# State-space tables made ahead and kept in DRAM, small matmuls of two pairs side by side, and a shorter final norm

## The chip, the cores and the metric

The kernel runs on one core of a Trainium2 chip. The metric is the device time of one execution in microseconds (us), the median over several runs. A trace of one profiled execution of the kernel before is at hand; its times count from the start of its span.

## The reference, cut to what matters

One layer of a streaming encoder over 512 tokens of width 2048: a projection, an attention that picks keys by an indexer, a state-space layer (S5) beside it, gates, an output projection, and a final RMSNorm. The parts that the change touches:

```python
bu_re = einsum("blgc,gpc->blgp", ug, bb_re)     # 32 groups: 16 channels in, 64 complex states each
bu_im = einsum("blgc,gpc->blgp", ug, bb_im)
# x[l] = lambda * x[l-1] + bu[l], lambda complex, one for each group and state
_, _, x_re, x_im = associative_scan(s5_combine, (lam_re, lam_im, bu_re, bu_im), axis=1)
y = einsum("blgp,gcp->blgc", x_re, c_re) - einsum("blgp,gcp->blgc", x_im, c_im) + d * ug
...
x = x + (gates[:, :, 0] * y_a + gates[:, :, 1] * y_b) @ w_out
out = x * rsqrt(mean(x * x, axis=-1) + EPS) * g_final
```

## The kernel before

Activations lie transposed in SBUF: features over the partitions, the 512 tokens along the free axis. Each large product runs as three matmuls in fp32r: high part by high part, low by high, high by low (lines 393 to 395; the output projection has its own, lines 646 to 648). A weight unit is 1 MB: SP loads it into one of three slots (`load`, line 299), ScalarE writes its high part (`w_hi`, line 673), VectorE the rest (`w_lo`, line 947). A unit of a projection is 48 matmuls of 128x512. All engines run orders written out by hand, tied by semaphores.

The stages follow each other on TensorE: indexer and q, k, v; `attgate` and `u` with the attention's small steps between their matmuls (35 steps, `attention_step`); `attout` (16 tiles of 24 matmuls, which ScalarE copies to `ya`); `merge0` (16 tiles of 48); `ssmgate`, `glu`, `ssmout`, `merge1`; `out` in two halves of 1024 columns.

The state-space layer runs inside `merge0`. Its 32 groups are 16 pairs; a pair fills 128 partitions (2 groups of 64 states). For pair j:

- `bu_of` on TensorE: six matmuls that contract over 32 rows (fp32r) into the two banks `pair_bank`, just ahead of a tile.
- VectorE turns the result back by the angle of each token (four products with the table `e_tab` of cosines and sines, two sums), scans along the tokens with the magnitude alone (`tensor_tensor_scan`, twice), and turns it forward again (four products, two sums) into `x_ri`.
- `y_of` on TensorE: two plain fp32 matmuls of 128 rows by 32 columns into a 32-partition strip of `sum_bank`, in the middle of a tile.

The table of pair j+1 is made during pair j by doubling: `e_start` copies 32 columns of `e_base`, and `e_double` goes 32 to 64 to 128 to 256 to 512. ScalarE makes the products with the sine (`e_scale`, line 840), VectorE two `scalar_tensor_tensor` for each doubling (lines 1228 and 1229). GpSimd multiplies each `merge0` gate into `ya` (line 376).

At the end, as each bank of the second half of `out` is done, VectorE adds it to the residual `res` (line 1352), ScalarE squares it (line 919), and for each tile t of 128 tokens the inverse norm is found (lines 922, 923, 1335). Then VectorE scales and weights 1344 of the 2048 columns (line 1337), while GpSimd weights the other 704 (line 383) for ScalarE to scale (line 907). SP sends both parts out (lines 344 and 346).

## Time and profile before

| | |
|---|---|
| Median of 3 runs | 1221.36 us (1220.9 to 1221.44) |
| The profiled execution's own time | 1219.88 us |
| Its span | 1218.0 us |
| TensorE busy | 1188.4 us (98%) |
| VectorE busy | 728.1 us (60%) |
| ScalarE busy | 417.3 us (34%) |
| GpSimd busy | 42.9 us (4%) |
| Mean granted TensorE clock | 0.997 of full |

The span is what the trace covers; the execution's own time is 1.88 us longer, and the median of the runs is 1.48 us above that. The profile names groups of instructions by line and tile. A matmul's row gives the time until its end, 0.39 us for 128x512, while the next starts 0.23 us later, so what a matmul costs in a full stream is read from start to start.

### The profile page before, as it was taken

The page shows a single profiled execution, that of the slowest core. Times are in us where ns is not written, and L with a number is a line of the kernel's source. Part 1 is how long each engine was busy: PE and PEld are TensorE (multiplying, and loading weights), DVE is VectorE, ACT ScalarE, POOL GpSimd, SP SyncE. Part 2 cuts the span into 40 slices and gives each one's busy share as a digit, 9 for nine tenths or more (in the row PEclk, how much of TensorE's full clock was granted, in tenths as well). Part 3 has the DMA queues.
Part 4 walks back from the last instruction along what each step waited for, and adds up shares of the span by engine and source line. Part 5 has one row for each costly group of instructions (what it writes and reads, how often), then busy time and mean ns, then how long its engine had stood idle before and what let it go on. Part 6 is the DMA issues. An engine that isn't in the chain of part 4 may idle for free.

```text
span 1218.0 us, 13219 instructions
## 1 busy us (share of the span) xinstructions
PE 1188.4 (98%) x5357; PEld 959.2 (79%) x5357; DVE 728.1 (60%) x1253; ACT 417.3 (34%) x558; POOL 42.9 (4%) x32
## 2 busy tenths in 40 slices
PE   5999999999999999999999999999999999999996
PEld 4999888887777888876666666788888888887885
DVE  5887479999456452469999999543223343523224
ACT  7432333323355432233233424233321222313114
POOL 3000000000000000000101011000000000000002
PEclk9999999999999999999999999999999999999998
DMA  7344232333221143322222222233333333255323
GB/s 241 104 120 122 71 100 73 80 93 104 69 70 36 51 116 104 104 72 77 80 78 75 69 70 69 70 104 104 95 81 102 104 104 91 85 175 204 103 70 138
DMA packets 167276, 118.07 MB, mean 97 GB/s; under 512 B 10456, under 2 KB 158256, under 8 KB 166064
## 3 DMA queue, kind: packets, MB, share of 16 engines
q1 hardware_dynamic: 160608, 116.34, 33.1%
q10 hardware_dynamic: 6608, 0.90, 0.4%
q8 instruction: 42, 0.69, 0.2%
q14 instruction: 18, 0.15, 0.0%
HBM read 113.03 MB, written 4.19 MB: 96 GB/s over the span
## 4 chain that ended last, share of the span: by engine, by line
PE 84%; DVE 12%; ACT 2%; DMA 1%; issue 1%; POOLq 0%; SPq 0%; DVEq 0%; ACTq 0%
PE bank L393 21%; PE bank L394 20%; PE bank L395 20%; PE bank L646 4%; PE bank L647 4%; PE bank L648 4%; DVE w_lo L947 2%; DVE score L1052 2%; DVE small L1051 2%; PE bank L545 1%; PE bank L526 1%; PE bank L583 1%; PE bank L584 1%; DVE score L1040 1%; DMA xt<-in_x 1%; PE bank L598 1%
## 5 line engine op out<-in xcount | busy, mean ns | idle before, releaser
L393 PE MATMUL bank<-act_hi,w_hi 128*128 128x512 f32 (+1 forms) x1088 | 424.5, 390 | 2.7 <-DVE w_lo L947 2.7
L394 PE MATMUL bank<-act_lo,w_hi 128*128 128x512 f32 (+1 forms) x1088 | 417.3, 384 | 0.0
L395 PE MATMUL bank<-act_hi,w_lo 128*128 128x512 f32 (+1 forms) x1088 | 417.0, 383 | 0.0
L947 DVE TENSOR_TENSOR w_lo<-w_raw,w_hi 128x2048 fp32r<-128x2048 f32 x96 | 219.8, 2290 | 195.6 <-ACT w_hi L673 194.7
L393 PEld LDWEIGHTS bank<-act_hi,w_hi 128*128 128x128 f32 x1088 | 204.3, 188 | 58.1 <-issue 19.2
L395 PEld LDWEIGHTS bank<-act_hi,w_lo 128*128 128x128 f32 x1088 | 204.3, 188 | 38.7
L394 PEld LDWEIGHTS bank<-act_lo,w_hi 128*128 128x128 f32 x1088 | 204.5, 188 | 34.2
L673 ACT ACTIVATE w_hi<-w_raw 128x2048 fp32r<-128x2048 f32 (+1 forms) x97 | 184.5, 1902 | 106.4 <-DMA w_raw<-in_w_out 105.3
L840 ACT ACTIVATE e_prod<-e_tab,rot 128x64 f32<-128x64 f32 (+1 forms) x64 | 31.8, 496 | 149.9 <-DVE e_tab L1229 90.9
L646 PE MATMUL bank<-w_hi,act_hi 128*128 128x512 f32 x192 | 74.7, 389 | 0.0
L647 PE MATMUL bank<-w_lo,act_hi 128*128 128x512 f32 x192 | 74.7, 389 | 0.0
L648 PE MATMUL bank<-w_hi,act_lo 128*128 128x512 f32 x192 | 74.7, 389 | 0.0
L1324 DVE TENSOR_TENSOR gate<-gate,yb 128x512 f32<-128x512 f32 x16 | 11.1, 692 | 97.3 <-ACT gate L679 97.3
L679 ACT ACTIVATE gate<-bank,g_cols 128x512 f32<-128x512 f32 x16 | 11.0, 688 | 134.1 <-PE bank L395 134.1
L743 ACT ACTIVATE relu<-bank 128x256 f32<-128x256 f32 (+2 forms) x48 | 23.6, 491 | 90.9 <-PE bank L494 84.7
L393 PE MATMUL bank<-a_hi,w_hi 128*128 128x512 f32 x128 | 49.9, 390 | 0.0
L395 PE MATMUL bank<-a_hi,w_lo 128*128 128x512 f32 x128 | 49.8, 389 | 0.0
L394 PE MATMUL bank<-a_lo,w_hi 128*128 128x512 f32 x128 | 49.8, 389 | 0.0
L376 POOL TENSOR_TENSOR ya<-ya,gate 128x512 f32<-128x512 f32 x16 | 23.3, 1457 | 710.0 <-ACT gate L852 710.0
L1040 DVE SCALAR_TENSOR_TENSOR score<-relu,w_idx,score 128x256 f32<-128x256 f32 (+2 forms) x45 | 27.8, 618 | 28.9 <-ACT relu L743 27.8
L646 PEld LDWEIGHTS bank<-w_hi,act_hi 128*128 128x128 f32 x192 | 36.0, 188 | 7.5
L647 PEld LDWEIGHTS bank<-w_lo,act_hi 128*128 128x128 f32 x192 | 36.0, 188 | 7.5
(241 smaller groups left out, 1383.5 us busy)
## 6 DMA issues: line engine op xcount, KB each, us to landing
w_raw<-in_w_in SPq DMA_DIRECT2D x68, 1024.0 KB, 5.6
w_raw<-in_w_out SPq DMA_DIRECT2D x16, 1024.0 KB, 5.5
w_raw<-in_w_att_out SPq DMA_DIRECT2D x8, 1024.0 KB, 5.5
xt<-in_x SPq DMA_DIRECT2D x4, 1024.0 KB, 7.9
w_raw<-in_w_ssm_out SPq DMA_DIRECT2D x4, 1024.0 KB, 5.1
res<-in_x SPq DMA_DIRECT2D x4, 1024.0 KB, 11.5
out_dram<-res SPq DMA_DIRECT2D x4, 672.0 KB, 3.1
out_dram<-res SPq DMA_DIRECT2D x4, 352.0 KB, 3.4
```

Source lines behind the costliest of these rows:

```text
L393: nc.tensor.matmul(out_ap, wh, x_hi[k], start=(j == 0), stop=False)
L394: nc.tensor.matmul(out_ap, wh, x_lo[k], start=False, stop=False)
L395: last = nc.tensor.matmul(out_ap, wl, x_hi[k], start=False, stop=(j == n - 1))
L646: nc.tensor.matmul(out_ap, mh, w_hi[:, slot, w], start=(k == 0), stop=False)
L647: nc.tensor.matmul(out_ap, mh, w_lo[:, slot, w], start=False, stop=False)
L648: last = nc.tensor.matmul(out_ap, ml, w_hi[:, slot, w], start=False, stop=(k == KD - 1))
L673: nc.scalar.activation(w_hi[:, u % SLOTS, 0:n_el], w_raw[:, u % SLOTS, 0:n_el], ACT.Copy).then_inc(high_done, 1)
L840: nc.scalar.activation(e_prod[:, :, 0:n], e_tab[:, j % 2, :, 0:n], ACT.Copy, scale=rot[:, 1, 4 + i, j:j + 1]).then_inc(e_scaled, 1)
L947: v.tensor_tensor(w_lo[:, u % SLOTS, :], w_raw[:, u % SLOTS, :], w_hi[:, u % SLOTS, :].bitcast(F32), ALU.subtract).then_inc(split_done, 1)
L1040: ins = v.scalar_tensor_tensor(scores[b], r, w, scores[b], ALU.mult, ALU.add)
L1051: link(v.max(small[:, 12:20], scores[b]))
L1052: link(v.match_replace(scores[b], small[:, 12:20], scores[b], REPLACED))
```

## The change

Tables. `e_base` is built ahead of the attention's first step. The tables of pairs 0 to 7 are made during the attention's steps, one doubling a step (`e_point`), ScalarE and VectorE sharing the work as before. Those of pairs 8 to 15 are made whole by VectorE at the start of `attout` (`e_whole`). ScalarE's queue stores each table in DRAM (`store_e`, 512 KB), and in `merge0` SP loads them back (`load_e`).

Small matmuls. `bu_of` and `y_of` work for two pairs at a time, every second tile, their matmuls alternating between the pairs: in `bu_of` the two pairs have different strips of 32 rows and different banks, in `y_of` different strips of 32 output columns. `x_ri` has two buffers. VectorE takes over GpSimd's gate product.

Final norm. The last two weight units are taken together, so that banks are done one at a time with 12 matmuls each. VectorE scales the first 1024 columns, weighted ahead in the first half, and weights the other 1024 while ScalarE squares; ScalarE scales them. GpSimd has no part.

```diff
+        e_prod = at("e_prod", r1 + 22 * KB, [2, SEQ // 2])
+        e_made = [at("e_made0", r1 + 28 * KB, [2, SEQ]), at("e_made1", r4, [2, SEQ])]
+            def load_e(j):
+                if j >= 2:
+                    sp.wait_ge(x_ready, j - 1)
+                else:
+                    sp.wait_ge(tile_done, TILE0["merge0"])
+                sp.dma_start(e_tab[:, j % 2, :, :], e_dram[j]).then_inc(e_loaded[j % 2], 16)
+            for stored_ in e_stored:
+                sp.wait_ge(stored_, 16 * PAIRS // 2)
+            for n, u in enumerate([*units("merge0"), *units("ssmgate")]):
+                load(u, KD, w_in_cols(COL_MERGE + P * n if n < KD else COL_SG + P * (n - KD)))
+                if n == 2:
+                    load_e(0)
+                    load_e(1)
+                if 4 <= n < PAIRS + 2:
+                    load_e(n - 2)
...
-            for j in range(KD):
-                pool.wait_ge(tile_free, TILE0["merge0"] + j + 1)
-                pool.tensor_tensor(ya[:, j, :], ya[:, j, :], gate[:, j % 2, :], ALU.mult).then_inc(gate_used, 1)
...
             def y_of(j):    
-                pe.wait_ge(x_ready, j + 1)
-                nc.tensor.matmul(out_ap, c_w[:, 0, q, 32 * jj:32 * jj + 32], x_ri[:, 0, :], start=True, stop=False)
-                nc.tensor.matmul(out_ap, c_w[:, 1, q, 32 * jj:32 * jj + 32], x_ri[:, 1, :], start=False, stop=True
+                pe.wait_ge(x_ready, j + 2)
+                for r in range(2):
+                    for p in (0, 1):
+                        cols_ = slice(32 * (jj + p), 32 * (jj + p) + 32)
+                        last = nc.tensor.matmul(sum_bank[q % 2][cols_, :], c_w[:, r, q, cols_], x_ri[:, p, r, :],
+                                                start=(r == 0), stop=(r == 1))
             def bu_of(j):
-                if j >= 1:
+                if j >= 2:
                     pe.wait_ge(bu_used, j)
...
-                if 1 <= n <= PAIRS:
+                if n % 2 == 1 and n < PAIRS:
                     bu_of(n - 1)
-                                              lambda k: y_of(n - 2) if k == KD // 2 and 2 <= n <= PAIRS + 1 else None)
+                                              lambda k: y_of(n - 3) if k == KD // 4 and n % 2 == 1 and 3 <= n <= PAIRS + 1 else None)
...
+            def store_e(j):
+                act.wait_ge(e_grown, 5 * (j + 1) if j < E_EARLY else 4 * E_EARLY + j + 1)
+                act.dma_start(e_dram[j], e_made[j % 2][:, :, :]).then_inc(e_stored[j % 2], 16)
+            def e_point(n):
+                if n % len(E_LEVELS) == 0 and n:
+                    store_e(n // len(E_LEVELS) - 1)
+                if n < len(E_LEVELS) * E_EARLY:
+                    j, l = n // len(E_LEVELS), E_LEVELS[n % len(E_LEVELS)]
+                    act.wait_ge(e_grown, n + j + 1)
+                    nc.scalar.activation(e_prod[:, :, 0:2 ** l], e_made[j % 2][:, :, 0:2 ** l], ACT.Copy, scale=rot[:, 1, l - 1, j:j + 1]
+                                         ).then_inc(e_scaled, 1)
...
+                act.wait_ge(bank_taken, 8 + 2 * t + 2)
+                link(nc.scalar.activation(square_out[:, 0, :], res[:, t, HALF + 512:D], ACT.Square, accum_out=small[:, 176 + t:177 + t]))
+                nc.scalar.activation(small[:, 184 + t:185 + t], small[:, 176 + t:177 + t], ACT.Sqrt, bias=small[:, 180 + t:181 + t],
+                                     scale=1.0 / D).then_inc(squares_done, 1)
                 act.wait_ge(scale_ready, t + 1)
+                nc.scalar.activation(res[:, t, HALF:D], fin[:, t % 2, :], ACT.Copy, scale=small[:, 188 + t:189 + t]
...
+            def e_whole(j):
+                er, ei = e_made[j % 2][:, 0, :], e_made[j % 2][:, 1, :]
+                dve.wait_ge(e_stored[j % 2], 16 * (j // 2))
+                link(v.tensor_copy(e_made[j % 2][:, :, 0:E_BASE], e_base[:, :, j, :]))
+                for l in E_LEVELS:
+                    n_, rr, ri = 2 ** l, rotors[l][0][:, j:j + 1], rotors[l][1][:, j:j + 1]
+                    link(v.tensor_scalar(e_prod[:, :, 0:n_], e_made[j % 2][:, :, 0:n_], ri, None, ALU.mult))
+                    a = mark(v.scalar_tensor_tensor(er[:, n_:2 * n_], er[:, 0:n_], rr, e_prod[:, 1, 0:n_], ALU.mult, ALU.subtract))
+                    last = v.scalar_tensor_tensor(ei[:, n_:2 * n_], ei[:, 0:n_], rr, e_prod[:, 0, 0:n_], ALU.mult, ALU.add)
+            e_whole(E_EARLY)
+            e_whole(E_EARLY + 1)
+            for i in (0, 1, 2):
+                low_through(UNIT0["attout"] + i + 2)
+                e_whole(E_EARLY + 2 * i + 2)
+                e_whole(E_EARLY + 2 * i + 3)
...
-                if nxt:
-                    e_double(j + 1, 5)
+                dve.wait_ge(tile_free, TILE0["merge0"] + j + 1)
+                v.tensor_tensor(ya[:, j, :], ya[:, j, :], gate[:, j % 2, :], ALU.mult).then_inc(gate_used, 1)
...
+                v.tensor_scalar(res[:, t, 0:HALF], res[:, t, 0:HALF], small[:, 188 + t:189 + t], None, ALU.mult).then_inc(final_done, 1)
```

In TensorE's order, this is where the first `bu_of` stands in the kernel before, between a tile into bank 1 and the next into bank 0 (banks 2 and 3 are `pair_bank`):

```order
L395 MATMUL bank1<-act_hi_49,w_lo_52 128x512
L598 MATMUL bank2<-u_hi_96,b_hi_87 128x512
L599 MATMUL bank2<-u_lo_97,b_hi_87 128x512
L600 MATMUL bank2<-u_hi_96,b_lo0_115 128x512
L598 MATMUL bank3<-u_hi_96,b_hi_87 128x512
L599 MATMUL bank3<-u_lo_97,b_hi_87 128x512
L600 MATMUL bank3<-u_hi_96,b_lo1_86 128x512
L393 MATMUL bank0<-act_hi_49,w_hi_53 128x512
```

The same place in the changed kernel (banks 4 and 5 are `turn_bank`, which take the second pair):

```order
L616 MATMUL bank2<-u_hi_97,b_hi_90 128x512
L616 MATMUL bank4<-u_hi_97,b_hi_90 128x512
L618 MATMUL bank2<-u_lo_98,b_hi_90 128x512
L618 MATMUL bank4<-u_lo_98,b_hi_90 128x512
L620 MATMUL bank2<-u_hi_97,b_lo0_116 128x512
L620 MATMUL bank4<-u_hi_97,b_lo0_116 128x512
L616 MATMUL bank3<-u_hi_97,b_hi_90 128x512
L616 MATMUL bank5<-u_hi_97,b_hi_90 128x512
L618 MATMUL bank3<-u_lo_98,b_hi_90 128x512
L618 MATMUL bank5<-u_lo_98,b_hi_90 128x512
L620 MATMUL bank3<-u_hi_97,b_lo1_89 128x512
L620 MATMUL bank5<-u_hi_97,b_lo1_89 128x512
```

Twelve matmuls of two pairs stand where six of one pair stood, and the place ahead of the following tile is empty.

The end of TensorE's order in the kernel before, the last two of the eight banks:

```order
L646 MATMUL bank6<-w_hi_53,act_hi_49 128x512
L647 MATMUL bank6<-w_lo_52,act_hi_49 128x512
L648 MATMUL bank6<-w_hi_53,act_lo_50 128x512
L646 MATMUL bank6<-w_hi_53,act_hi_49 128x512
L647 MATMUL bank6<-w_lo_52,act_hi_49 128x512
L648 MATMUL bank6<-w_hi_53,act_lo_50 128x512
L646 MATMUL bank7<-w_hi_53,act_hi_49 128x512
L647 MATMUL bank7<-w_lo_52,act_hi_49 128x512
L648 MATMUL bank7<-w_hi_53,act_lo_50 128x512
L646 MATMUL bank7<-w_hi_53,act_hi_49 128x512
L647 MATMUL bank7<-w_lo_52,act_hi_49 128x512
L648 MATMUL bank7<-w_hi_53,act_lo_50 128x512
```

In the changed kernel twelve matmuls go into bank 7 there, after twelve into bank 6; so the last but one bank is done twelve matmuls ahead of the end, not six.

On ScalarE's order, the start of `attout` in the changed kernel (L709 copies a tile to `ya`, L808 is a store of `store_e`); before, the copies and the `w_hi` stand there alone:

```order
L709 ACTIVATE ya<-bank 128x512
L703 ACTIVATE w_hi<-w_raw 128x2048
L808 DMA e_tables<-e_made_117 128x1024
L709 ACTIVATE ya<-bank 128x512
L808 DMA e_tables<-e_made_118 128x1024
L709 ACTIVATE ya<-bank 128x512
```

Each of the first eight copies now has a store behind it, which waits for VectorE's table, so the next copy waits for that too.

## Rows read from the trace of the kernel before

**Rows 1.** The page, busy time and share of the span, TensorE.

```profile
PE 1188.4 (98%) x5357; PEld 959.2 (79%) x5357; DVE 728.1 (60%) x1253; ACT 417.3 (34%) x558; POOL 42.9 (4%) x32
```

**Rows 2.** Timeline of TensorE around one `bu_of`: start us, us, engine, line, operation.

```profile
620.09 0.39 PE L395 MATMUL bank<-act_hi,w_lo 128*128 128x512 f32 x1
...
620.41 0.49 PE L598 MATMUL bank<-u_hi,b_hi 32*128 32x512 f32 x1
...
621.99 0.19 PEld L393 LDWEIGHTS bank<-act_hi,w_hi 128*128 128x128 f32 x1 [0.36 <-issue]
621.99 0.50 PE L393 MATMUL bank<-act_hi,w_hi 128*128 128x512 f32 x1
622.10 0.19 PEld L394 LDWEIGHTS bank<-act_lo,w_hi 128*128 128x128 f32 x1
...
622.33 0.39 PE L394 MATMUL bank<-act_lo,w_hi 128*128 128x512 f32 x1
```

**Rows 3.** Timeline of TensorE around one `y_of`.

```profile
628.02 0.39 PE L395 MATMUL bank<-act_hi,w_lo 128*128 128x512 f32 x1
...
628.34 1.04 PE L583 MATMUL bank<-x_ri,c_w 128*32 128x512 f32 x2
629.22 1.02 PE L584 MATMUL bank<-x_ri,c_w 128*32 128x512 f32 x2
...
630.51 0.40 PE L394 MATMUL bank<-act_lo,w_hi 128*128 128x512 f32 x1
```

**Rows 4.** Timeline of VectorE: one pair from its first product to its last doubling.

```profile
622.20 0.69 DVE L1255 TENSOR_TENSOR prod<-bank,e_tab 128x512 f32<-128x512 f32 x1 [0.26 <-PE bank L600]
622.81 0.68 DVE L1256 TENSOR_TENSOR prod<-bank,e_tab 128x512 f32<-128x512 f32 x1
...
635.59 0.48 DVE L1229 SCALAR_TENSOR_TENSOR e_tab<-e_tab,rot,e_prod 128x256 f32<-128x256 f32 x1
```

**Rows 5.** Groups by line, VectorE, 529.9 to 766.6: busy us, mean ns, idle before.

```profile
L1229 DVE SCALAR_TENSOR_TENSOR e_tab<-e_tab,rot,e_prod 128x32 f32<-128x32 f32 (+3 forms) x60 | 20.2, 337 | 0.0
```

**Rows 6.** Timeline of the attention's steps, in brackets idle time and what ended it.

```profile
352.17 1.28 ACT L762 ACT_TABLE_LOAD   x1 [0.69 <-DVE small L1144]
...
354.38 0.71 PE L545 MATMUL bank<-pT,v_tok 128*128 128x128 f32 x4 [1.34 <-ACT pT L772]
...
400.15 0.49 DVE L1152 TENSOR_SCALAR probs<-probs,small 128x512 f32<-128x512 f32 x1
```

**Rows 7.** Attention's window: PE, PEld, DVE, ACT, POOL busy, clock, DMA share, GB/s.

```profile
314.00:434.00 120.00, 118.50 (x628) 96.67 (x627) 62.69 (x208) 58.00 (x122) 0.00 (x0) 1.00 0.19 54
```

**Rows 8.** The page, ScalarE's group for the tables.

```profile
L840 ACT ACTIVATE e_prod<-e_tab,rot 128x64 f32<-128x64 f32 (+1 forms) x64 | 31.8, 496 | 149.9 <-DVE e_tab L1229 90.9
```

**Rows 9.** Timeline of VectorE: the attention's first step, and later `e_base`, first and last.

```profile
324.06 0.29 DVE L1141 CUSTOM_DVE_ANT_0 probs<-bank,bias 128x128 f32<-128x128 f32 x1 [9.72 <-PE bank L526]
...
502.70 0.07 DVE L1192 MEMSET e_base<- 128x16 f32 x1
...
511.46 0.42 DVE L1096 TENSOR_TENSOR e_base<-b_raw 128x256 f32<-128x256 f32 x1
```

**Rows 10.** Timeline of VectorE in `attout`: its first work after the last unit of `u`.

```profile
445.78 0.43 DVE L1096 TENSOR_TENSOR b_bar<-b_raw,par 128x256 f32<-128x256 f32 x1 [12.75 <-DMA parity<-in_c_parity]
```

**Rows 11.** Timelines of all engines at the end of the span.

```profile
1181.53 2.29 DVE L947 TENSOR_TENSOR w_lo<-w_raw,w_hi 128x2048 fp32r<-128x2048 f32 x1 [8.43 <-ACT w_hi L673]
...
1206.42 0.39 PE L648 MATMUL bank<-w_hi,act_lo 128*128 128x512 f32 x1
...
1208.13 1.28 DVE L1352 TENSOR_TENSOR res<-bank,res 128x512 f32<-128x512 f32 x2
...
1210.68 0.29 ACT L923 ACTIVATE small<-small 128x1 f32<-128x1 f32 x1
...
1214.43 0.88 ACT L907 ACTIVATE res<-rest,small 128x704 f32<-128x704 f32 x1 [2.69 <-POOL rest L383]
...
1215.34 0.33 SPq L346 DMA_DIRECT2D out_dram<-res  x1
```

More of the change, by code:

```diff
@@ L41 @@
     int(c) for c in np.cumsum((0,) + WIDTHS[:-1]))
-V_COLS = 1344
+HALF = D // 2
 UNIT = 2048
@@ L71 @@
              ("u", 0): range(10, 18), ("u", 1): range(18, 27), ("u", 2): range(27, 35)}
+E_LEVELS = range(5, 9)
+E_EARLY = PAIRS // 2
 def split12(x):
@@ L620, in _, with out_bank @@
                     unit(u, i)
+            def out_bank(half, t, n, ks):
+                for k in ks:
+                    if half == 0 and (k, t, n) == (0, 0, 0):
+                        pe.wait_ge(tile_free, TILE0["out"])
+                    if half == 1 and k == 0:
+                        pe.wait_ge(bank_taken, 2 * t + n + 1)
+                    slot = (UNIT0["out"] + 8 * half + k // 2) % SLOTS
+                    out_ap = banks[2 * t + n][:, :]
+                    m_hi, m_lo = (s_hi, s_lo) if k < QUADS else (act_hi, act_lo)
+                    mh, ml = m_hi[:, k, t * P:(t + 1) * P], m_lo[:, k, t * P:(t + 1) * P]
+                    w = slice(k % 2 * 1024 + n * 512, k % 2 * 1024 + n * 512 + 512)
+                    nc.tensor.matmul(out_ap, mh, w_hi[:, slot, w], start=(k == 0), stop=False)
+                    nc.tensor.matmul(out_ap, mh, w_lo[:, slot, w], start=False, stop=False)
+                    last = nc.tensor.matmul(out_ap, ml, w_hi[:, slot, w], start=False, stop=(k == KD - 1))
+                return last
@@ new lines, in _ @@
+                    for k in (2 * c, 2 * c + 1):
+                        for t in (1, 2, 3, 0):
+                            for n in range(2):
+                                last = out_bank(half, t, n, (k,))
+                    last.then_inc(tile_done, 1)
+                if half == 0:
+                    wait_split(UNIT0["out"] + 7)
+                    pe.wait_ge(m_low, KD)
+                    for t in range(TOK):
+                        for n in range(2):
+                            last = out_bank(half, t, n, (14, 15))
+                            last.then_inc(bank_done if (t, n) != (TOK - 1, 1) else tile_done, 1)
+                else:
+                    wait_split(LAST_UNIT - 1)
+                    for t in range(TOK):
+                        for n in range(2):
+                            out_bank(half, t, n, range(12, KD)).then_inc(bank_done, 1)
@@ L1130, in _, with spread @@
             low_through(UNIT0["attgate"] + 6)
+            def spread(col, n_):
+                return col.unsqueeze(2).to_broadcast([P, PAIRS, n_])
+            link(v.memset(e_base[:, 0, :, 0:1], 1.0))
+            link(v.memset(e_base[:, 1, :, 0:1], 0.0))
+            for l in range(5):
+                n_ = 2 ** l
+                er, ei = e_base[:, 0, :, 0:n_], e_base[:, 1, :, 0:n_]
+                rr, ri = spread(rotors[l][0], n_), spread(rotors[l][1], n_)
+                ta, tb = e_temp[:, 0, :, 0:n_], e_temp[:, 1, :, 0:n_]
+                tt(ta, er, rr, ALU.mult)
+                tt(tb, ei, ri, ALU.mult)
+                tt(e_base[:, 0, :, n_:2 * n_], ta, tb, ALU.subtract)
+                tt(ta, er, ri, ALU.mult)
+                tt(tb, ei, rr, ALU.mult)
+                tt(e_base[:, 1, :, n_:2 * n_], ta, tb, ALU.add)
```

273 lines of the change are left out of this document (121 added, 152 removed).

## The prediction

> **What bounds the kernel now.** First the page: TensorE is busy 98% of the span [rows 1]. So only three things can move the time: matmul time taken off TensorE's stream, waits put into it, and what lies behind its last matmul. Next TensorE's timeline inside `merge0`. In the full stream a matmul costs 0.2275 us from start to start. Around a `bu_of` the reader is to see more than six such steps: from the last matmul before it to the second after it pass 2.24 us where two steps would take 0.455, so a `bu_of` costs 1.785 us: six steps (1.365) and 0.42 for going into and out of the small form [rows 2]. A `y_of` costs 2.49 - 0.455 = 2.035 us: each fp32 matmul is two records, each 0.44 from the next, so 1.74 for four, and 0.295 for the two changes of form [rows 3]. Sixteen of each make 28.6 + 32.6 = 61.1 us, with TensorE never idle there. Last the timelines at the end: the last matmul ends at T = 1206.81, the span at 1218.0, 11.2 us later [rows 11].
>
> All sums are made against the profiled execution, 1219.9 us; the median of the runs is 1.5 us above it, and I forecast that median. A change under 0.2% (2.4 us) can't be told from none.
>
> **Part 1: `bu_of` for two pairs.** The eight places left cost between two bounds. If matmuls on different strips of 32 rows run at once, a double group costs what a single one does, 1.785. If they don't, twelve steps and the change of form cost 3.15, and only the saved change counts. The trace shows no two such matmuls side by side. It does show that weight loads follow each other at 0.11 us [rows 2]; two loads, 0.22, just fit into a step of 0.2275, so only the first load of the second pair shows. I take 1.785 + 0.11 = 1.9, since no resource in the rows is needed twice: other rows of the array, other partitions, other banks. 28.6 - 8 x 1.9 = **-13.4** (bounds -14.3 and -3.4).
>
> **Part 2: `y_of` for two pairs.** Here the strips are output columns. The order is A, B, A, B, but each matmul is two records. If records start in order and those of one strip can't overlap, then A1 runs alone, A2 beside B1, B2 beside A1', A2' beside B1', and B2' alone: five steps of 0.44 for eight records, 2.475 with the change of form. Full overlap gives 2.035, none 3.78. I take the five steps: 32.6 - 8 x 2.475 = **-12.8** (bounds -16.3 and -2.4).
>
> For both parts the Trainium skill speaks in "TensorE: Matmul & The Clock Gate", Part 3: small matmuls on different row or column strips run at once, four row tiles 3.07 times and three column tiles 2.38 times as fast as one after another, and a pack takes about one matmul and 4 ns for each further tile. No row here shows that. By this rule both double groups would cost what single ones do, and the sum below would come out 4.4 us lower, at 1188.
>
> **Part 3: VectorE in `merge0`.** If it falls behind, `y_of` waits for `x_ready`. Now a pair takes 13.87 us from first product to the end of the last doubling [rows 4]. Out go eight `scalar_tensor_tensor`, each 0.337 less the 0.08 by which neighbours overlap [rows 4, 5], 2.06 together, and the copy, 0.1. In come the gate product, 0.6, and 0.1 as the wait for `x_ready` now stands right behind the last sum. Spread over the pairs, u's low parts and `y_of_quad` add 0.24. That is 12.65, for two pairs 25.3; TensorE will take 2 x 48 x 0.2275 + 1.9 + 2.475 = 26.2. VectorE stays just under it. From the end of a `bu_of` to the `y_of` that needs its result TensorE has two tiles, the next `bu_of` and 15 matmuls, 27.1 us. So **0**; without this cover each 0.1 us that a pair takes over 13.1 costs 1.6 us. The gate product waits for ScalarE's sigmoid of tile j, whose matmuls end before VectorE comes to it; behind it are queued the scans, and `y_of` behind those. The loads of tables go through SP's queue between weight loads: table j waits for pair j-2 done, a whole pair (12.65 us) ahead of its use, and the weight load queued behind it isn't due for two tiles.
>
> **Part 4: tables during the attention.** Half of ScalarE's 31.8 us for tables [rows 8] and as much on VectorE move here, where in 120 us VectorE is busy 63 and ScalarE 58 [rows 7]. There is room on average. But a step is a chain over three engines, and at one place TensorE already waits 1.34 us, behind a table load of 1.28 on ScalarE [rows 6]. There one step's additions, 0.5 on ScalarE and 0.6 on VectorE, come on top, with a few tenths at other steps: **+1.3**. Bounds: 0, and 1.1 us at each of five steps where a weight's high and low parts stand between, 5.5. `e_base` takes 502.70 to 511.88, 9.2 us, and moves into VectorE's idle 9.72 us ahead of the first step [rows 9]: 0; uncovered it would cost up to 9.2.
>
> **Part 5: eight tables in `attout`.** One is a copy, four `tensor_scalar` (0.49 for the longest [rows 6]) and eight `scalar_tensor_tensor` in a chain, some 4.1 us by these rows. VectorE is idle from 433.0 for 12.75 us [rows 10]; two tables go there. The others need stores, which ScalarE issues only behind its nine loads and its copies. A store takes about 2.7 us (the last of the kernel, 1215.34 to 1218.0 [rows 11]), so table 10 starts near 450, and with three `w_lo` between, the last is done near 478. ScalarE copies one tile per 24 matmuls, 5.45 us, and waits for one table each, 4.1 to 5.2: it keeps up, and TensorE has a second bank. **0**. Late next would be `w_lo` of `attout`'s sixth unit, behind the tables and `b_bar`, about 485 against 488. If stores and tables went strictly one after another (7.3 us each against 5.45), it would cost 15.
>
> **Part 6: the end.** Last bank done at T; add 0.69; from the last add's end to the root's end are 1.56 us now [rows 11], of which the sum of four squares (0.3) moves ahead: T + 2.0. Reciprocal 0.15; then VectorE's product, at most 0.98 (twice 0.49 [rows 6]), beside ScalarE's, 1024 columns at 0.88 per 704, 1.28: T + 3.4. Now GpSimd holds ScalarE up to 1214.43, T + 7.6 [rows 11]. The last transfers are 512 KB twice; one of 352 KB took 2.66 us, two in a row would be 5.3; I take 3.8. End at T + 7.2 instead of 11.2: **-4.0** (bounds -2.6 and -5.2). The last unit's low part is ready at 1183.82 [rows 11]; now it is wanted 96 matmuls before the end, at 1185.0: hidden, with 1.2 us to spare.
>
> **Sum.** -13.4 - 12.8 + 1.3 - 4.0 = -28.9: 1191.0 against 1219.9, as a median **1192.5**. Its own range is 1187 to 1198.
>
> **Rivals.**
> - *Only the row strips overlap*, the column strips don't, as each streams all 128 partitions and in fp32. `y_of` then saves 2.4, not 12.8: 1203. 0.13.
> - *Nothing overlaps* (the change doesn't do what it says): -3.4 - 2.4 + 1.3 - 4.0 = -8.5, 1213. For it: no row shows overlap. 0.12.
> - *Every change of strip costs like a change of form*, and the time ends above. Entering the small form costs about 0.11 above a step (620.41 comes 0.32 after 620.09; 622.33 comes 0.34 after 621.99 [rows 2]). A double `bu_of` changes strip twelve times, a double `y_of` four times, 128 in all, 14.1 us, against 5.8 that fewer changes of form save: +8.3 + 1.3 - 4.0 = +5.6, 1227. It decides from 0.066 us a change on. Against it: in the rows the cost stands only where the shape changes. 0.06.
> - *VectorE becomes the bound* of `merge0`: at 13.5 us a pair, 1.6 x 4 = 6.4 us, 1199. Against it: it waits for TensorE even now with more work [rows 4]. 0.06.
> - *A wait in `attout` or the attention* at its upper bound: 1197 to 1207. 0.04.
>
> To the third rival the Trainium skill says in "TensorEngine Tiling (Array Packing)", Key Properties, that changing the tiling mode drains the engine, changing the tile does not. The 0.11 us at the changes of form agrees; the other half no row shows. By this rule the rival falls and the forecast stands.
>
> **How the numbers follow.** The forecast has 0.59. It and the rivals up to 1207 hold 0.82, but some of the forecast's own chance lies outside its range, so the range goes on to the case without overlap: 1186 to 1213.5. Faster: all but the third rival, 0.93; within 0.2%: 0.02; slower: 0.05.
>
> **What the profile after would show.** Right: matmuls of `bu_of` in twos some 0.1 us or less apart, twos 0.23 apart, a group of 1.9 us; `y_of` 2.5; TensorE without waits in `merge0`; `scalar_tensor_tensor` of the tables in the attention and a wait of TensorE of some 3 us there in all; the span's end 7.2 us behind the last matmul. Wrong: starts at even 0.23 steps through a double group (no overlap), or at 0.34 (rival three); waits of TensorE for `x_ri` (VectorE the bound) or for `ya` in `attout`.

## Result and the profile after

| | before | after |
|---|---|---|
| Median | 1221.13 us (1220.59 to 1221.44, 4 runs) | 1187.24 us (1186.81 to 1188.11, 4 runs) |
| Span of the profiled execution | 1218.0 us | 1185.0 us |
| Last matmul's end, and from there to the end of the span | 1206.81, 11.2 us | 1177.66, 7.3 us |

The ratio is 0.9724, 95% interval 0.9707 to 0.9741: 33.9 us faster. The forecast was 1192.5, with a range of 1186 to 1213.5; the time lies 5.3 us under the one and near the lower end of the other. Of the span's 33.0 us, 29.1 lie ahead of the last matmul's end and 3.9 behind it.

The page after, to be held against [rows 1]:

```profile
PE 1158.0 (98%) x5357; PEld 949.8 (80%) x5357; DVE 752.5 (64%) x1317; ACT 403.4 (34%) x526; POOL 11.8 (1%) x12
```

TensorE has the same 5357 matmul instructions and is busy 30.4 us less. It is still the bound, at 98%.

TensorE's timeline around one double `bu_of`, against [rows 2] (start us, us, engine, line, operation; x2 means two records):

```profile
584.79 0.39 PE L407 MATMUL bank<-act_hi,w_lo 128*128 128x512 f32 x1
585.11 0.51 PE L616 MATMUL bank<-u_hi,b_hi 32*128 32x512 f32 x2
585.44 0.40 PE L618 MATMUL bank<-u_lo,b_hi 32*128 32x512 f32 x2
585.68 0.40 PE L620 MATMUL bank<-u_hi,b_lo 32*128 32x512 f32 x2
585.91 0.40 PE L616 MATMUL bank<-u_hi,b_hi 32*128 32x512 f32 x2
...
586.69 0.51 PE L405 MATMUL bank<-act_hi,w_hi 128*128 128x512 f32 x1
587.03 0.40 PE L406 MATMUL bank<-act_lo,w_hi 128*128 128x512 f32 x1
```

The matmuls come in twos, twos 0.23 to 0.24 apart, and from the last large matmul to the second after the group pass 2.24 us, exactly as around a single one before. Less two steps, 0.455, the group costs 1.785. The second pair is free. Its weight loads (PEld) run beside those of the first as well; the first two:

```profile
585.11 0.18 PEld L616 LDWEIGHTS bank<-u_hi,b_hi 32*128 32x128 f32 x2 [0.35 <-issue]
```

Around a double `y_of`, against [rows 3]:

```profile
590.01 0.39 PE L407 MATMUL bank<-act_hi,w_lo 128*128 128x512 f32 x1
590.33 1.91 PE L597 MATMUL bank<-x_ri,c_w 128*32 128x512 f32 x8
592.17 0.50 PE L405 MATMUL bank<-act_hi,w_hi 128*128 128x512 f32 x1
592.51 0.40 PE L406 MATMUL bank<-act_lo,w_hi 128*128 128x512 f32 x1
```

Eight records in 1.91 us, where four took as long before; 2.50 - 0.455 = 2.045 us a group, against 2.035 for a single one. Neither an input that takes all 128 partitions nor plain fp32 stands in the way of the overlap.

TensorE's timeline at the attention's places that wait now, in brackets the idle time and what ended it (before there was 1.34 at 354.38 [rows 6] and 0.16 at 352.60, and nothing at 340; a fourth wait now, 0.18 at 376.90, isn't shown):

```profile
340.74 0.49 PE L557 MATMUL bank<-pT,v_tok 128*128 128x128 f32 x2 [0.62 <-ACT pT L802]
...
354.47 0.44 PE L547 MATMUL bank<-ident,probs 128*128 128x128 f32 x2 [0.88 <-DVE probs L1249]
355.86 0.71 PE L557 MATMUL bank<-pT,v_tok 128*128 128x128 f32 x4 [0.95 <-ACT pT L802]
```

The end, against [rows 11], in the timeline of all engines:

```profile
1177.27 0.39 PE L657 MATMUL bank<-w_hi,act_lo 128*128 128x512 f32 x1
1177.76 0.69 DVE L1392 TENSOR_TENSOR res<-bank,res 128x512 f32<-128x512 f32 x1 [1.22 <-PE bank L657]
...
1179.90 1.15 ACT L965 ACTIVATE res<-fin,small 128x1024 f32<-128x1024 f32 x1 [0.30 <-DVE small L1421]
1179.90 0.75 DVE L1424 TENSOR_SCALAR res<-res,small 128x1024 f32<-128x1024 f32 x1
...
1181.07 0.41 SPq L369 DMA_DIRECT2D out_dram<-res  x1
```

Both products start together 2.2 us behind the last matmul's end (T + 2.2), where ScalarE had to wait for GpSimd until T + 7.6 before. The last transfer is issued at T + 3.4 and lands 3.9 us later.

### The profile page after: what moved, and what is told of

It reads as the page before. It is cut to its first block, busy times and chain, and to the rows that moved or that the text cites. A ratio compares the mean times of both kernels' runs of the same rounds, so it can differ in the third digit from the quotient of the medians.

```text
span 1185.0 us, 13271 instructions
## 1 busy us (share of the span) xinstructions
PE 1158.0 (98%) x5357; PEld 949.8 (80%) x5357; DVE 752.5 (64%) x1317; ACT 403.4 (34%) x526; POOL 11.8 (1%) x12
## 4 chain that ended last, share of the span: by engine, by line
PE 83%; DVE 13%; DMA 1%; ACT 1%; issue 1%; SPq 0%; DVEq 0%; ACTq 0%
PE bank L405 21%; PE bank L407 20%; PE bank L406 20%; PE bank L655 5%; PE bank L657 5%; PE bank L656 5%; DVE w_lo L992 3%; DVE score L1097 2%; DVE small L1096 2%; PE bank L557 1%; PE bank L597 1%; PE bank L538 1%; DVE score L1085 1%; DMA xt<-in_x 1%; PE bank L547 1%
## 5 line engine op out<-in xcount | busy, mean ns | idle before, releaser
L709 ACT ACTIVATE gate<-bank,g_cols 128x512 f32<-128x512 f32 x16 | 11.0, 688 | 134.1 <-PE bank L407 134.1
L773 ACT ACTIVATE relu<-bank 128x256 f32<-128x256 f32 (+2 forms) x48 | 23.6, 492 | 90.9 <-PE bank L506 84.7
L657 PEld LDWEIGHTS bank<-w_hi,act_lo 128*128 128x128 f32 x192 | 36.0, 188 | 7.4
L405 PE MATMUL bank<-s_hi,w_hi 128*128 128x512 f32 x80 | 31.1, 389 | 0.0
```

The lines of the kernel that those rows point to most:

```text
L405: nc.tensor.matmul(out_ap, wh, x_hi[k], start=(j == 0), stop=False)
L657: last = nc.tensor.matmul(out_ap, ml, w_hi[:, slot, w], start=False, stop=(k == KD - 1))
L773: nc.scalar.activation(relu[:, n % 2, 0:(b + 1) * P], pair_bank[n % 2][:, 0:(b + 1) * P], ACT.Relu, scale=IDX_DIM ** -0.5).then_inc(relu_d ...
```

## Experiments

Each run's time is a median; the kernel before was timed beside each and had 1220.85 to 1221.25 there, so differences of up to 0.4 us between runs say nothing.

### 1. The two pairs one after another in `bu_of`

```diff
-                for r in range(2):
-                    for p in (0, 1):
-                        nc.tensor.matmul(into[p][r][:, :], b_hi[rows[p], r, q, :], u_hi[rows[p], :], start=True, stop=False)
-                    for p in (0, 1):
+                for p in (0, 1):
+                    for r in range(2):
+                        nc.tensor.matmul(into[p][r][:, :], b_hi[rows[p], r, q, :], u_hi[rows[p], :], start=True, stop=False)
                         nc.tensor.matmul(into[p][r][:, :], b_hi[rows[p], r, q, :], u_lo[rows[p], :], start=False, stop=False)
-                    for p in (0, 1):
```

> The changed kernel, but bu_of gives out the six matmuls of the first pair and then the six of the second, so that neighbours in TensorE's order are on the same strip of 32 rows (only the sixth and the seventh differ). Theory (neighbours on different strips run at once, and nothing looks further ahead): eleven steps of 0.2275 in place of six, a double group of 1.785 + 5 x 0.2275 = 2.92, eight of them +9.1 us, 1196.3. Rival (what counts is that the two pairs stand in one group, whatever the order, because the engine finds the other strip's work itself): 1.785 as before the edit, 1187.2.

Measured: 1192.03, +4.8 us; half of the one, and not the other. TensorE's timeline of one group:

```profile
586.24 0.39 PE L407 MATMUL bank<-act_hi,w_lo 128*128 128x512 f32 x1
586.56 0.49 PE L616 MATMUL bank<-u_hi,b_hi 32*128 32x512 f32 x1
586.89 0.39 PE L617 MATMUL bank<-u_lo,b_hi 32*128 32x512 f32 x1
587.13 0.39 PE L618 MATMUL bank<-u_hi,b_lo 32*128 32x512 f32 x1
587.13 0.62 PE L616 MATMUL bank<-u_hi,b_hi 32*128 32x512 f32 x2
587.48 0.50 PE L617 MATMUL bank<-u_lo,b_hi 32*128 32x512 f32 x2
587.71 0.50 PE L618 MATMUL bank<-u_hi,b_lo 32*128 32x512 f32 x2
587.94 0.39 PE L616 MATMUL bank<-u_hi,b_hi 32*128 32x512 f32 x1
...
589.05 0.40 PE L406 MATMUL bank<-act_lo,w_hi 128*128 128x512 f32 x1
```

The group costs 2.81 - 0.455 = 2.355, so 0.57 or two and a half steps more than the changed kernel's, 4.6 for eight groups. In program order the lines go L616, L617, L618 over and over; here two L616 start before an L617, so a matmul of the second pair, the seventh of the group, was taken ahead. It starts with the third, at 587.13. The fourth comes a step later, at 587.36, which is why that row is 0.62 long and not 0.39. The seventh has thus passed three matmuls, the fourth to the sixth. From there the second pair runs beside the first, about half a step off, and its last three (from 587.94) are alone. So matmuls of another strip don't have to be neighbours; they are taken ahead, but only so far: the seventh didn't start with the first.

### 2. The same in `y_of`

```diff
-                for r in range(2):
-                    for p in (0, 1):
+                for p in (0, 1):
+                    for r in range(2):
```

> The changed kernel, but y_of gives out both matmuls of the first pair (r = 0, 1) and then both of the second. Theory, from the records of the changed kernel, where the two passes of a fp32 matmul run beside the two passes of its neighbour: the first alone (2 steps), the second beside the third (2), the last alone (2), six steps of 0.44 instead of four, a double group of 2.045 + 0.88 = 2.93, eight of them +7.0 us, 1194.3. The prediction's rule (records start in order, those of one strip never overlap): seven steps, +10.5 us, 1197.7. No overlap left at all: eight steps, +14.1 us, 1201.3. Nothing lost: 1187.2.

Measured: 1187.51, within 0.3 us of the changed kernel: nothing is lost. Its timeline:

```profile
590.61 0.39 PE L407 MATMUL bank<-act_hi,w_lo 128*128 128x512 f32 x1
590.93 1.92 PE L597 MATMUL bank<-x_ri,c_w 128*32 128x512 f32 x8
592.78 0.50 PE L405 MATMUL bank<-act_hi,w_hi 128*128 128x512 f32 x1
```

Eight records in 1.92 us though the first pair's two matmuls stand ahead of the second pair's. The second pair's first matmul has only one to pass, or three records, as each matmul is two; experiment 1 had three passed as well. Both rules that let only neighbours share a step, mine before the run and that of the prediction, are refuted.

### 3. Three, three, three, three in `bu_of`

```diff
                 for r in range(2):
                     for p in (0, 1):
                         nc.tensor.matmul(into[p][r][:, :], b_hi[rows[p], r, q, :], u_hi[rows[p], :], start=True, stop=False)
-                    for p in (0, 1):
                         nc.tensor.matmul(into[p][r][:, :], b_hi[rows[p], r, q, :], u_lo[rows[p], :], start=False, stop=False)
-                    for p in (0, 1):
                         last = nc.tensor.matmul(into[p][r][:, :], b_lo[r][rows[p], q, :], u_hi[rows[p], :], start=False, stop=True)
```

> The changed kernel, but bu_of gives out three matmuls of the first pair, three of the second, three of the first, three of the second. Theory, from the run with six and six, where the seventh matmul started together with the fourth (a matmul of another strip starts up to three places ahead of its turn): the fourth starts with the first, nothing is lost, 1187.2, with the records in twos through the whole group. Rival (only neighbours overlap, and the start of the seventh with the fourth had another cause): at each of the three seams one step is shared, nine steps in place of six, 3 x 0.2275 x 8 = +5.5 us, 1192.7.

Measured: 1188.20, +1.0. The rival's +5.5 is out. TensorE's timeline:

```profile
586.09 0.51 PE L616 MATMUL bank<-u_hi,b_hi 32*128 32x512 f32 x2
586.42 0.41 PE L617 MATMUL bank<-u_lo,b_hi 32*128 32x512 f32 x2
586.65 0.41 PE L618 MATMUL bank<-u_hi,b_lo 32*128 32x512 f32 x2
586.89 0.40 PE L616 MATMUL bank<-u_hi,b_hi 32*128 32x512 f32 x2
```

All in twos, so the fourth starts with the first and passes two. (The expectation put the seventh of experiment 1 beside the fourth; it starts with the third, but the three places hold, as it passes three matmuls.) The extra 1.0 us isn't in the group, which costs 1.79 to 1.80 in all eight places; the profiled execution has it long before, at the head, where the indexer's first product comes at 108.1 against 107.0, in code that is the same. The head differs like this between the profiled executions of all kernels here, 106.9 to 108.3; the last section shows where it arises. Whether the median of this one is up by the same cause isn't shown.

### 4. One pair at a time, with all the rest of the change

```diff
-                if n % 2 == 1 and n < PAIRS:
+                if 1 <= n <= PAIRS:
                     bu_of(n - 1)
-                                              lambda k: y_of(n - 3) if k == KD // 4 and n % 2 == 1 and ...
+                                              lambda k: y_of(n - 2) if k == KD // 2 and 2 <= n <= PAIRS + 1 else None)
```

> The changed kernel with its tables, its buffers and banks and its final norm, but bu_of and y_of for one pair at a time, at every tile, as in the kernel before. Theory (all the gain of merge0 is eight bu_of and eight y_of that cost nothing beside their neighbours): sixteen of 1.785 and sixteen of 2.035 where eight of 1.785 and eight of 2.045 stand, +14.3 + 16.2 = +30.5 us, 1217.7, and no wait of TensorE in merge0. Rival (part of the gain came from the tables or from VectorE's shorter pair): less than that, under 1215.

Measured: 1218.58, +31.3 over the changed kernel, 2.7 under the kernel before. Tables, buffers and final norm together are worth 2.7 us (3.9 won at the end, experiment 7, and 1.2 to 1.8 lost in the attention, experiment 8); the overlap of the small matmuls is worth all the rest. Of the 0.8 us above the forecast some 0.5 is in what a window of two steps doesn't catch: behind each small group the first large matmuls still come 0.23 to 0.24 apart, not 0.2275 (before, behind a `y_of`: 630.51, 630.75, 630.99, 631.22, 631.46). Taken over ten matmuls instead of two, a `bu_of` costs 0.02 more and a `y_of` 0.04. The rest is not explained.

### 5. `y_of` for four pairs, every fourth tile, with four buffers for `x_ri`

```diff
-                pe.wait_ge(x_ready, j + 2)
+                pe.wait_ge(x_ready, j + 4)
...
                 for r in range(2):
-                    for p in (0, 1):
+                    for p in range(4):
```

> The changed kernel, but y_of for four pairs at once, every fourth tile, four strips of 32 output columns side by side, with four buffers for x_ri. Theory (four strips overlap as two do): a group of 8 matmuls costs 2.05 as one of 2 or 4 does, four groups in place of eight, -8.2 us, 1179.0; VectorE, 25.4 us for two pairs against TensorE's 24.7, lags by some 3 us in the end, and the later places of y_of take that up. Rival (only two strips at a time overlap, or the input of each strip has to come by in turn): eight steps of 0.44, a group of 3.8, four of them 15.2 against 16.4, -1 us, 1186. Second rival (VectorE becomes the bound): some 3 to 5 us of the gain are lost, 1182 to 1184, with waits of TensorE for x_ri.

Measured: 1180.30 (1179.67 to 1180.55), ratio to the kernel before 0.9665 (0.9651 to 0.9680), 6.9 us under the changed kernel. TensorE's timeline of one group (the four pairs' inputs have three names):

```profile
590.18 0.39 PE L413 MATMUL bank<-act_hi,w_lo 128*128 128x512 f32 x1
590.50 0.62 PE L603 MATMUL bank<-x_ri,c_w 128*32 128x512 f32 x2
590.51 0.62 PE L603 MATMUL bank<-x,c_w 128*32 128x512 f32 x1
590.51 0.62 PE L603 MATMUL bank<-x_3r,c_w 128*32 128x512 f32 x1
590.95 0.60 PE L603 MATMUL bank<-x_ri,c_w 128*32 128x512 f32 x2
...
592.69 0.40 PE L412 MATMUL bank<-act_lo,w_hi 128*128 128x512 f32 x1
```

Sixteen records in four steps; 2.51 - 0.455 = 2.055 us a group, so four groups save 8.1. The spans differ by 6.5; the head of this execution is 0.9 longer (the indexer's first product at 108.0), and the waits for `res` and `w_lo` are 0.6 longer. The trace shows no wait for `x_ri`, but VectorE has no idle time left in `merge0` here (19.93 to 19.97 busy in every 20 us from 560 to 740), and that does cost TensorE something, in another place than the second rival named:

```profile
732.20 0.50 PE L411 MATMUL bank<-act_hi,w_hi 128*128 128x512 f32 x1 [0.38 <-DVE w_lo L998]
```

ScalarE had written that weight's high part at 728.50, but VectorE came to the low part only at 729.86, behind a pair's products. The changed kernel has no such wait in `merge0`.

### 6. Small matmuls together, tables still made in `merge0`

```diff
-        x_ri = take("x_ri", [2, SEQ])
+        x_ri = take("x_ri", [2, 2, SEQ])
...
-                if 1 <= n <= PAIRS:
+                if n % 2 == 1 and n < PAIRS:
                     bu_of(n - 1)
...
                 if nxt:
                     e_double(j + 1, 7)
-                if j:
-                    dve.wait_ge(y_done, j)
-                v.tensor_tensor(x_ri[:, 0, :], p0, p1, ALU.subtract)
+                if j >= 2:
+                    dve.wait_ge(y_done, j - 1)
+                v.tensor_tensor(x_ri[:, j % 2, 0, :], p1, p3, ALU.subtract)
```

> The kernel before, with bu_of and y_of for two pairs at a time (its matmuls alternating between the pairs, two buffers for x_ri, four banks), but the tables still made inside merge0 by ScalarE and VectorE, and the old final norm. Theory (making the tables ahead is what lets TensorE have the gain): VectorE needs some 13.87 us for a pair, 27.7 for two, against TensorE's 25.67, so TensorE waits for x_ri some 2 us every two tiles, 16 us in all, and only 14 of the 30.5 us arrive: 1207 (1204 to 1212). Rival (the tables didn't matter, VectorE has room enough): all 30.5, 1190.6.

Measured: 1213.90, 7.3 under the kernel before, half of the forecast 14 and above its range of 1204 to 1212. The chain of waits of TensorE, first row, and the waits themselves in its timeline:

```profile
PE bank L584 <- DVE x_ri L1292: 18.1, 7, 3.1
```

```profile
591.65 1.91 PE L584 MATMUL bank<-x_ri,c_w 128*32 128x512 f32 x8 [2.79 <-DVE x_ri L1292]
619.57 2.64 PE L584 MATMUL bank<-x_ri,c_w 128*32 128x512 f32 x8 [2.20 <-DVE x_ri L1292]
```

The mechanism is right, and its price too (18.1 us of waits against 16). But 30.5 - 18.1 is 12.4, not 7.3. What is missing is clock. Windows around the second of these waits (stretch, its length, PE busy, granted clock, share of DMA, GB/s):

```profile
619.00:620.00 1.00, 0.43 (x2) 1.00 0.00 0
620.00:621.00 1.00, 1.00 (x6) 0.81 0.00 0
621.00:622.00 1.00, 1.00 (x4) 0.50 0.00 0
...
624.00:625.00 1.00, 1.00 (x6) 0.99 0.00 0
```

Shortly after TensorE works again its granted clock falls to 0.50, that is 1.2 GHz, and comes back some 3.4 us later; the same eight records take 2.64 us instead of 1.91. Of the seven waits four have this behind them; at the last of them (3.10 us) the clock is down already when TensorE resumes. Windows around one with it and one without:

```profile
610.00:640.00 30.00, 27.80 (x120) 0.94 0.26 70
640.00:665.00 25.00, 22.17 (x102) 1.00 0.32 85
```

The three other stretches of 25 to 30 us with such a wait have 0.93 or 0.94 too: 1.7 to 1.8 us lost at each, 7 in all. 12.4 - 7 = 5.4, against 5.8 between the spans (1218.0 and 1212.2).

### 7. The new end alone, on the kernel before

```diff
-            pool.wait_ge(gf_loaded, 16)
-            for t in range(TOK):
-                pool.wait_ge(bank_taken, 8 + 2 * t + 2)
...
+                    for t in range(TOK):
+                        for n in range(2):
+                            out_bank(half, t, n, range(12, KD)).then_inc(bank_done, 1)
...
+                v.tensor_scalar(res[:, t, 0:HALF], res[:, t, 0:HALF], small[:, 188 + t:189 + t], None, ALU.mult).then_inc(final_done, 1)
```

> The kernel before with nothing but the new end: the last two weight units together, the split at 1024 columns, no part for GpSimd. Theory: the end comes 7.3 us behind the last matmul instead of 11.2, -3.9 us, 1217.3. Rival (the last but one unit's low part is late when both are taken together, and TensorE waits for it): less than 2 us are left, with a wait of TensorE for w_lo ahead of its last 96 matmuls.

Measured: 1217.32, -3.9. The last matmul ends at 1208.30, the span at 1215.6, 7.3 later. The span itself is only 2.4 shorter, as the head is 1.4 longer in this execution (the indexer's first product at 108.3 against 106.9).

### 8. Without the doublings in the attention, three times

```diff
-                    v.scalar_tensor_tensor(er[:, n_:2 * n_], er[:, 0:n_], rr, e_prod[:, 1, 0:n_], ALU.mult, ALU.subtract)
-                    v.scalar_tensor_tensor(ei[:, n_:2 * n_], ei[:, 0:n_], rr, e_prod[:, 0, 0:n_], ALU.mult, ALU.add
-                                           ).then_inc(e_grown, 1)
...
+                    if j < 2:
+                        link(v.memset(e_made[j % 2][:, :, :], 1.0))
```

> The changed kernel without the doublings of tables 0 to 7 during the attention: neither ScalarE's products nor VectorE's scalar_tensor_tensor are made there; the first 32 columns are still copied, two tables filled with ones once, and the stores remain. Eight of the tables are thereby not those of the reference. Theory (these additions on ScalarE and VectorE cost TensorE 1.2 us of waits in the attention): its waits there fall from 2.7 to 1.5 us, and the time by 1.2 us, 1186.0. Rival (the waits belong to the stores and the queue behind them, or are made up later): within 0.3 us of 1187.2.

Measured: 1187.18, no change, which looks like the rival. But TensorE's wait of 0.62 at 340.74 had become one of 1.05, and ahead of it VectorE's timeline has the experiment's own filling:

```profile
335.20 0.91 DVE L1197 MEMSET e_made<- 128x1024 f32 x1 [0.16 <-issue]
...
336.86 2.28 DVE L987 TENSOR_TENSOR w_lo<-w_raw,w_hi 128x2048 fp32r<-128x2048 f32 x1
```

It pushed the weight's low part, and the attention's chain behind that, back by about its own length: the low part starts 12.4 us behind the first product of queries and keys (324.5), where without a fill on VectorE (the third run below) it is 11.2. The trace's attention is 0.6 us shorter than the changed kernel's even so (90.4 us from the first to the last of these products, against 91.0), but the head of this execution is 0.8 longer. So the fill was moved ahead of the first step:

> As the changed kernel without the doublings of tables 0 to 7 in the attention, with the two fills of ones now ahead of the attention's first step, where VectorE is idle, and not 0.91 us long in front of a weight's low part. Eight tables are not those of the reference. Theory (the doublings cause the extra waits): TensorE's waits in the attention fall from 2.7 us to the 1.5 of before, the time by 1.2 to 1.9 us, to 1185.3 to 1186.0. Rival (the copies and the stores of 512 KB in ScalarE's queue cause them): waits stay at 2.6, the time at 1187.2.

Measured: 1186.83, -0.4, with waits of 2.1 us in the attention. Now the fills of 1.8 us weren't hidden there either: from the first product of queries and keys to the first of probabilities and values it took 8.6 us (323.9 to 332.5), against 7.6 in the changed kernel (323.8 to 331.4). Two waits for `probs` (0.28 and 0.35, at 329 and 332) are new, right behind the fills. The third time GpSimd made them:

```diff
+            for i in range(2):
+                pool.memset(e_made[i][:, :, E_BASE:SEQ], 1.0).then_inc(e_scaled, 1)
```

> As the changed kernel without the doublings of tables 0 to 7 in the attention; the two fills of ones are now GpSimd's, which is idle there, so that VectorE has neither doublings nor fills. Eight tables are not those of the reference. Theory (the extra 1.2 us of waits are the doublings'; in the two runs before, a fill of some 0.9 us or 1.8 us on VectorE took their place): from TensorE's first product of queries and keys to its last it takes 89.2 us as in the kernel before, not 91.0 as in the changed one, and the run takes 1185.5. Rival (copies and stores cost something by themselves): 90.4 or more between these two.

Measured: 1185.13, -2.1 (-1.9 if each is held against the kernel before beside it). The groups of TensorE's products of queries and keys (count, shortest, median and longest, first and last start), of the changed kernel and of this one:

```profile
L538 PE MATMUL bank<-kT,qT x64: 270/430/595, 323.8 to 414.8; 128*128 128x128 f32 x16, 128*128 128x256 f32 x16, 128*128 128x384 f32 x16, 128*128 128x512 f32 x16
```

```profile
L541 PE MATMUL bank<-kT,qT x64: 270/430/595, 323.9 to 413.1; 128*128 128x128 f32 x16, 128*128 128x256 f32 x16, 128*128 128x384 f32 x16, 128*128 128x512 f32 x16
```

91.0 us and 89.2, which is also what the kernel before takes. So the doublings cost 1.8 us, 1.2 of it as waits in TensorE's list (2.7 against 1.5); copies and stores cost nothing. How much of it is ScalarE's products and how much VectorE's share, this run doesn't tell, as it leaves out both.

### 9. Attempts to get these 1.8 us back, on the kernel of experiment 5

```diff
+E_POINTS = [s for s in range(35) if s not in (4, 9)]
...
-                if s <= len(E_LEVELS) * E_EARLY:
-                    e_point(s)
+                if s in E_POINTS:
+                    e_point(E_POINTS.index(s))
```

> The kernel with y_of for four pairs at once, and no doubling at steps 4 and 9 of the attention, the last of their tiles, ahead of which ScalarE's table loads wait; the 33 points of the tables spread over the other 33 of 35 steps. Theory (a doubling's 0.4 us on ScalarE ahead of the sigmoid's table load, and 0.4 us on VectorE ahead of the probabilities, are what TensorE waits for at these two places): waits in the attention fall from 2.7 to about 1.8 us, 1179.4 against 1180.3. Rival (the doubling at the step behind counts just as much): no change, 1180.3.

Measured: 1179.42 (1178.98 to 1180.12). The waits in the attention are 2.6 us against 2.7: the wait for `probs` grew to 2.1 and that for `pT` fell to 0.5. From the first to the last product of queries and keys it takes 90.9 us, against 91.0 before the edit. The 0.9 us under experiment 5 are no gain of this edit: the head is 0.5 shorter in the trace, and the kernel before, timed beside each, was 0.4 shorter too (1220.85 against 1221.24). The time is the rival's, but its reason isn't. At the two places that the edit frees, the waits did fall, from 2.5 us (0.64, 0.87 and 0.95) to 1.5, what they were before the change. In exchange a wait of 0.18 further on grew:

```profile
376.98 0.55 PE L554 MATMUL bank<-ident,probs 128*128 128x128 f32 x3 [0.89 <-DVE probs L1256]
```

As the points move on by two steps, a longest doubling (two times 0.48 us on VectorE from 375.43, then a copy) now stands ahead of the probabilities there, where a short one of two times 0.28 stood. That its length makes the wait is the plain reading of these rows; it wasn't tried by itself.

> The same, and VectorE makes its doublings behind a step's probabilities instead of ahead of them. Theory (the doublings' 0.4 us no longer stand in the chain to the transposes): waits of 1.5 us or less, 1179.0. Rival (ScalarE, whose product of the next doubling waits for VectorE's, is held up in its queue and the probabilities' exponentials behind it come late): more waits than 2.7 us, 1180.5 to 1185.

Measured: 1179.83 (1178.36 to 1181.75), too wide to tell from the last: two executions took 1178.4 and 1178.6, two 1181.1 and 1181.8, and the trace is of one of the first two. It has less waiting, 1.6 us, and 90.2 us between the two products, so in that execution VectorE's order is worth 0.7 us of the 1.8; what lengthens the other two isn't known. The best version is one of these, 41 us or 3.4% under the kernel before, 7 to 8 under the changed one.

## Why the prediction was right, and where not

- **What bounds.** Right: TensorE's stream and what lies behind it. Experiment 4 puts 31.3 of 33.9 us on the overlap.
- **Part 1, `bu_of`.** The mechanism was right, 14.3 us by the groups against 13.4. The term was mis-sized by the 0.11 for a second weight load, which doesn't show: it runs beside the first (two in 0.18 us at 585.11), and the group costs 1.785, its lower bound.
- **Part 2, `y_of`.** The gain is 32.6 - 8 x 2.045 = 16.2 instead of 12.8. The step that failed is "If records start in order and those of one strip can't overlap": the second half holds, the first doesn't. B1 starts with A1 (in experiment 5 the names tell the pairs apart: all four start at 590.50 or 590.51), and by experiments 1 to 3 the engine starts a matmul of another strip a few places ahead of its turn. Five steps are four. This is the larger part of the 5.3 us by which the forecast was high: 3.4 here, 0.9 in part 1, and 1.2 because the median stands 2.2 above the profiled span now, where 3.4 was assumed, less some 0.2 in the rest. That last part is luck of the executions and no merit or fault of the reasoning. The Trainium skill's rule, in "TensorE: Matmul & The Clock Gate", Part 3, was set aside for my own and would have given 1188. The trace agrees with it: 1.785 and 2.045 us for two tiles, 2.055 for four, against 1.785 and 2.035 for one.
- **Part 3, VectorE.** Right. In the changed kernel two pairs start 25.68 us apart (702.00 and 727.68) with 0.32 of waiting, so 12.7 a pair, 25.4 of work for two (25.3 forecast), under TensorE's 25.7, which came out shorter than the forecast 26.2. The room is 0.3 us, not 0.9. From the end of a `bu_of` to the `y_of` that needs it TensorE has 29.3 us (586.7 to 616.0), as the `y_of` that lies between was left out of the 27.1. The 0 holds, and experiment 6 shows what the cover is worth: without it 18 us of waits, and 7 of lost clock that no rival had counted. The fourth rival's price of 1.6 us for each 0.1 over TensorE's time is too low once the waits bring the clock down.
- **Part 4, the attention.** 1.3 forecast, 1.2 in the list of waits, 1.8 by experiment 8. The number is right, the place mostly isn't, and that is luck. At the place named, where 1.1 was to come on top, 0.88 + 0.95 stand where 0.16 + 1.34 stood: 0.3 more. The larger part, 0.62, came at 340.74, 14 us earlier, behind ScalarE's table load there (338.74), where the kernel before had no wait; 0.2 came at 376.90. And 0.6 of the 1.8 is in no wait at all. The table base stayed hidden.
- **Part 5, `attout`.** Right: a table takes 4.16 us against 4.1, the last ends at 480.3 (478 forecast), ScalarE's copies come every 5.44 us, and TensorE waits for nothing there.
- **Part 6, the end.** -3.9 in the trace against -4.0, -3.9 by experiment 7. VectorE's product took 0.75, not 0.98, ScalarE's 1.15, not 1.28, and the transfers 3.9.
- **The rivals.** "Only the row strips overlap", "nothing overlaps" and "every change of strip costs" fall with the records in twos, at every 0.23 us in `bu_of` and every 0.44 in `y_of`. To the last the Trainium skill's "TensorEngine Tiling (Array Packing)", Key Properties, had said that a change of the tile alone doesn't drain the engine; twelve changes of strip in a group that costs what one without them does agree.

The terms as measured, -14.3, -16.2, +1.2 (or 1.8) and -3.9, give -33.2 or -32.6 for a span shorter by 33.0. They would be 0.5 larger with what comes behind each small group (experiment 4), so they close to within about half a microsecond.

## What to carry to other kernels

Small matmuls that use a strip of 32 rows or 32 output columns cost nothing beside others of different strips: collect two (for output columns four were tried too) before issuing them, and give out those that are to run together at most three apart. At three apart nothing was lost, at six a third of a group's gain (0.57 of 1.785). What limits this here is not TensorE but who feeds it: when matmuls are saved, ask first whether the engine behind can keep the new pace, and reckon with lost clock on top of a wait of two or three microseconds. When work is spread over a chain of steps, keep the longest pieces away from the steps where TensorE has no slack: in experiment 9 it waited 0.2 us behind a short doubling and 0.9 behind a long one at the same step. When an experiment leaves work out, what is put in its place has a price too, and it must be on an idle engine before the result means anything.

## What was unexpected of the hardware

- TensorE starts a matmul of another strip ahead of matmuls that stand before it. In experiment 1 the seventh starts with the third and passes three; in experiment 3 the fourth starts with the first and passes two; in experiment 2 the third starts with the first and passes one, which is three records, and in experiment 5 the fourth pair's first record passes three others. More than three was never seen. Only experiment 1 shows a limit (the seventh could have started with the first); whether it is counted in matmuls stays open.
- Four strips of output columns in plain fp32, each streaming 128 partitions of its own input, run as fast as one (2.055 against 2.035 us).
- Of seven waits of TensorE in experiment 6 four came with a few us at half clock, those of 2.15, 2.19, 2.20 and 3.10 us, while those of 2.79, 2.83 and 2.83 had nothing behind them. The length of the wait alone doesn't decide it; what does stays open.
- The head of the kernel, in code that is the same, took up to 1.4 us longer in one profiled execution than in another. The traces show where. The same matmul of the head takes 0.63 us at first and 0.39 later, and the moment of the change differs from one execution to the next. In the kernel before, and in experiment 7:

```profile
22.70 0.39 PE L458 MATMUL bank<-act_lo,w_hi 128*80 128x512 f32 x1
```

```profile
23.14 0.63 PE L452 MATMUL bank<-act_lo,w_hi 128*80 128x512 f32 x1
```

  In the first the records are short from 22.7 on, in the second from 25.2 on, and the indexer's first product comes at 106.9 and 108.3. In all fourteen traces the head is longer by about half of what the change is later, to within 0.1 us. 0.63 is also what a matmul of 128x512 takes at half clock in experiment 6 (622.73), so this looks like the clock's rise at the start; the windows view itself gives 1.00 for this stretch, so it is read from the lengths alone. Up to 1.4 us in a comparison of two spans comes from this.
